# Two chained transformer blocks on one core: the value blocks of the memory, the filter products and the spectrum products each move one stage later

## The reference, cut to what matters

```python
# first block
x = x + 0.5 * rms(swiglu(rms(x, ffn1_pre_g), ffn1_w_gu, ffn1_w_down), ffn1_post_g)    # D_FF = 2816
...                                     # mixer: projections w_in (dt, xbc, q, k, v, z, gates) of rms(x, mix_pre_g),
mixed = (g_attn * attn_out + g_ssd * ssd_out) @ w_mix_out
x = x + rms(mixed, mix_post_g)
hq = rms(x, xa_pre_g)
qx = (hq @ xa_w_q)                                                     # 4 heads of 256
kx, vx = split(rms(mem, mem_norm_g) @ xa_w_kv, 2)                      # mem: 256 rows of 1024, an input
p = softmax(einsum('bqhd,bkhd->bhqk', qx, kx) * 256 ** -0.5)
x = x + rms(einsum('bhqk,bkhd->bqhd', p, vx) @ xa_w_o, xa_post_g)
x = x + 0.5 * rms(swiglu(rms(x, ffn2_pre_g), ffn2_w_gu, ffn2_w_down), ffn2_post_g)
# second block (Hyena and latent attention)
h = sin(freq_2 * (sin(freq_1 * (z @ w_f1 + b_f1)) @ w_f2 + b_f2))      # z: fixed positions
k = (h @ w_f3) * decay                                                 # filter taps, inputs alone
k_spec = rfft(both directions of k)                                    # used by the long convolution of Hyena
```

## Time and profile before

| | |
|---|---|
| median of 3 runs | 1103.66 us (1103.06 to 1103.74) |
| the profiled execution's own time | 1102.39 us |
| its span, first to last instruction | 1100.6 us |
| PE busy | 1085.5 us, 99% of the span, 8538 matmuls |
| DVE busy | 792.8 us, 72% |
| ACT busy | 590.7 us, 54% |
| the 16 DMA engines | 171 GB/s in the mean, 188.59 MB |
| mean granted TensorE clock | 1.000 |

### The profile page before, as it was taken

One profiled execution on the slowest core, in us unless ns is written; L12 is line 12 of the kernel. 1 busy time (PEld: TensorE's weight loads), 2 busy tenths in 40 slices (PEclk: granted clock), 3 DMA queues, 4 the chain that ended last, 5 costly groups with the idle time before them and its releaser, 6 DMA issues.

```text
span 1100.6 us, 21007 instructions
## 1 busy us (share of the span) xinstructions
PE 1085.5 (99%) x8538; PEld 1029.8 (94%) x8538; DVE 792.8 (72%) x1114; ACT 590.7 (54%) x844; POOL 0.2 (0%) x4
## 2 busy tenths in 40 slices
PE   9999999999999999999999999999999999999998
PEld 7999999999999999999999898999999798999998
DVE  5765555858998968777777867675555686997774
...
PEclk9999999999999999999999999999999999999999
...
DMA packets 29137, 188.59 MB, mean 171 GB/s; under 512 B 3496, under 2 KB 4809, under 8 KB 7370
## 3 DMA queue, kind: packets, MB, share of 16 engines
...
...
## 4 chain that ended last, share of the span: by engine, by line
PE 84%; DVE 9%; ACT 4%; issue 2%; DMA 1%; SPq 0%; ACTq 0%; DVEq 0%
PE bank L515 14%; PE bank L514 14%; PE bank L516 14%; PE bank L526 10%; PE bank L527 10%; PE bank L528 10%; DVE sb_w_lo L2017 3%; PE bank L613 2%; ACT sb_w_hi L1331 2%; PE bank L857 1%; PE bank L739 1%; PE bank L687 1%; DVE sb_hT_lo L2094 1%; DMA sb_w_raw<-in_w 1%; PE bank L1178 1%
## 5 line engine op out<-in xcount | busy, mean ns | idle before, releaser
L2017 DVE TENSOR_TENSOR sb_w_lo<-sb_w_raw,sb_w_hi 128x2048 fp32r<-128x2048 f32 x169 | 386.5, 2290 | 152.3 <-ACT sb_w_hi L1331 152.0
L1331 ACT ACTIVATE sb_w_hi<-sb_w_raw 128x2048 fp32r<-128x2048 f32 x169 | 322.8, 1910 | 34.5 <-PE bank L516 33.0
L514 PE MATMUL bank<-sb_hT_hi,sb_w_hi 128*128 128x256 f32 (+1 forms) x816 | 225.9, 277 | 0.0
L516 PE MATMUL bank<-sb_hT_hi,sb_w_lo 128*128 128x256 f32 (+1 forms) x816 | 225.8, 277 | 0.0
L515 PE MATMUL bank<-sb_hT_lo,sb_w_hi 128*128 128x256 f32 (+1 forms) x816 | 225.7, 277 | 0.0
L526 PE MATMUL bank<-sb_hT_hi,sb_w_hi 128*128 128x256 f32 (+2 forms) x744 | 213.4, 287 | 2.1 <-DVE sb_w_lo L2017 1.1
L527 PE MATMUL bank<-sb_hT_lo,sb_w_hi 128*128 128x256 f32 (+2 forms) x744 | 206.3, 277 | 0.0
L528 PE MATMUL bank<-sb_hT_hi,sb_w_lo 128*128 128x256 f32 x744 | 206.0, 277 | 0.0
L514 PEld LDWEIGHTS bank<-sb_hT_hi,sb_w_hi 128*128 128x128 f32 (+1 forms) x816 | 152.7, 187 | 0.1
L516 PEld LDWEIGHTS bank<-sb_hT_hi,sb_w_lo 128*128 128x128 f32 (+1 forms) x816 | 152.7, 187 | 0.1
L515 PEld LDWEIGHTS bank<-sb_hT_lo,sb_w_hi 128*128 128x128 f32 (+1 forms) x816 | 152.6, 187 | 0.1
...
## 6 DMA issues: line engine op xcount, KB each, us to landing
...
```

The source lines that it names most:

```text
L514: pe.matmul(o, a_hi, b_hi, start=first, stop=False)
L516: return pe.matmul(o, a_lo, b_hi, start=False, stop=last)
L1331: act.activation(w_hi[b % STAGES][:], w_raw[b % RING][:], ACT.Copy).then_inc(w_hi_in, 1)
L2017: tt(w_lo[b % STAGES][:], w_raw[b % RING][:], f32(w_hi[b % STAGES][:]), ALU.subtract).then_inc(w_lo_in, 1)
```

## The change

- **Weight list and keys.** The stage xa_kv of 8 blocks becomes xa_k (4 blocks, after FFN1) and xa_v (4 blocks, between mix_out and xa_q). After FFN1 PE runs kv0, kv1, kv2, `norm_turn(2)`, kv3, dt. The value blocks kv4 to kv7 stand after mix3, two on either side of `raw_turn(3)`.
- **Memory kept.** After the key blocks' hi and lo parts are used, a DVE add (128 x 2048) writes mem_T = hi + lo, and ACT waits for it before the copy of dt. In the first mixer, ahead of mix_out, ACT rounds it to late_hi and DVE subtracts to late_lo.
- **Filter.** The eight filter products move from the seam mix to xa to the seam xa to FFN2; all eight spectrum products from there and from after FFN2 to the seam FFN2 to second mixer, six ahead of `raw_turn(5)` and two behind it.
- **DVE.** `norm_rows(1)` moves from behind tile 3 of FFN1 to between tiles 20 and 21. The folds leave the cross attention: `filter_fold(0, 0..3)` stand behind tiles 0, 1, 2, 3 of FFN2 (in place of `spectrum_pair(0, *)`), `filter_fold(1, 0..2)` between tiles 20 and 21, `filter_fold(1, 3)` behind 21. In the second mixer `norm_low(6)` and `low_after(ckv)` come ahead of `spectrum_pair(1, *)`, and `spectrum_pair(0, *)` stands after `low_after(z_hy + 3)`.
- **Order after FFN1 on DVE.** Lower kv2, `norm_rows(2)`, lower kv3, `norm_low(2)`, lower dt, the add of mem_T, lower xbc0. Before it was: lower kv2 and kv3, `norm_rows(2)`, lower kv4 to kv7, `norm_low(2)`, lower the rest.
- **Small ones.** The load of the transform matrix (dft_f) on ACT's queue moves behind `post_gain(3)`; half buffers and dft_f lie elsewhere; `WIDER` has other entries.

Cut to its core (a line of "..." marks what is left out):

```diff
     ffn(1)
-    plain("xa_kv", "xa_w_kv", 0, 8)
+    plain("xa_k", "xa_w_kv", 0, 4)
...
     plain("mix_out", "w_mix_out", 0, 4)
+    plain("xa_v", "xa_w_kv", 4 * 256, 4)
     plain("xa_q", "xa_w_q", 0, 4)
...
-WIDER = {**dict.fromkeys(("xbc1", "xbc10", "qkv1", "qkv7", "gate0", "gate2", "gate3", "gate4", "ssd5", "attn3.0", "zz3",
-                          "gg6", "gg7", "hyo1.0"), (2, 2)),
-         **dict.fromkeys(("kv5", "qkv8", "qkv9", "qkv10", "gate6", "ssd7", "xaq2", "xaq3", "hy4"), (8, 8)),
-         "ckv": (2, 0), "xo2": (8, 0), "out2": (8, 0)}
+WIDER = {**dict.fromkeys(("xbc1", "xbc10", "xbc11", "qkv1", "gate0", "gate2", "gate3", "gate4", "ssd5", "ssd7", "attn3.0",
+                          "zz3", "gg6", "gg7", "hyo1.0"), (2, 2)),
+         **dict.fromkeys(("qkv9", "qkv10", "xaq2", "xaq3"), (4, 4)),
+         **dict.fromkeys(("qkv7", "qkv8", "gate6", "hy4"), (8, 8)),
+         "xo2": (4, 0), "ckv": (8, 0), "out2": (4, 0)}
...
         mem_lo = place(90, "mem_lo", [P, KD, SEQ], F32R)
+        mem_T = place(8, "mem_T", [P, KD, SEQ])
+        late_hi = place(32, "late_hi", [P, KD, SEQ], F32R)
+        late_lo = place(40, "late_lo", [P, KD, SEQ], F32R)
...
-        dft_f = place(0, "dft_f", [P, 4, P])
-        half = place(32, "half", [P, 2, 4, HY])
+        dft_f = place(56, "dft_f", [P, 4, P])
+        half = [place(0, "half0", [P, 4, HY]), place(40, "half1", [P, 4, HY])]
...
-            for i in range(8):
-                if i < 4:
-                    feature_block(f"kv{i}", FIRST["xa_kv"] + i, 2, mem_hi, mem_lo, ready=None if i else norm_done(1))
-                else:
-                    token_block(f"kv{i}", FIRST["xa_kv"] + i, 256, mem_hi, mem_lo)
-                if i == 4:
+            for i in range(4):
+                feature_block(f"kv{i}", FIRST["xa_k"] + i, 2, mem_hi, mem_lo, ready=None if i else norm_done(1))
+                if i == 2:
                     norm_turn(2, mix_xn, 2)
...
-            xq = FIRST["xa_q"]
-            for i in range(6):
-                filter_taps(i, (3, 4, 5, 6, xq % 3, (xq + 1) % 3)[i])
+            def value_block(h):
+                if h == 0:
+                    pe.wait_ge(S("late_lo"), 1)
+                token_block(f"kv{4 + h}", FIRST["xa_v"] + h, 256, late_hi, late_lo)
+            value_block(0)
+            value_block(1)
             raw_turn(3, x_added(1))
-            for i in (6, 7):
-                filter_taps(i, (xq + 2) % 3 if i == 6 else (xq + 1) % 3)
-            for i in range(8):
+            value_block(2)
+            value_block(3)
+            for i in range(4):
                 wait_read(pe, f"kv{i}")
...
-            filter_spectrum(0, (3, 4, 5, 6))
+            up = FIRST["ffn2"]
+            for i in range(6):
+                filter_taps(i, (3, 4, 5, 6, up % 3, (up + 1) % 3)[i])
             raw_turn(4, x_added(2))
+            for i in (6, 7):
+                filter_taps(i, (up + 2) % 3 if i == 6 else (up + 1) % 3)
             ffn_part(2, 4)
-            filter_spectrum(1, (0, 1, 2, 7))
+            at = (0, 1, 2, 7, (FIRST["cq"] + 1) % 3, (FIRST["cq"] + 2) % 3)
+            for i in range(6):
+                filter_spectrum(i, at[i])
             raw_turn(5, x_added(3))
+            for i in (6, 7):
+                filter_spectrum(i, at[i - 2])
...
-            for i in range(8):
-                if i == 2:
+            for i in range(4):
+                if i == 1:
                     act.wait_ge(S("x_ready"), X_READY[0] - 2)
                     norm_squares(x, mix_xn)
                 o = full(act, f"kv{i}")
-                if i < 4:
-                    copy(f"kv{i}", xa_k[:, 2 * i:2 * i + 2, :], two(o))
-                else:
-                    copy(f"kv{i}", xa_v[:, :, (i - 4) * 256:(i - 3) * 256], two(o))
-                after(FIRST["xa_kv"] + i)
-                if i == 4:
+                copy(f"kv{i}", xa_k[:, 2 * i:2 * i + 2, :], two(o))
+                after(FIRST["xa_k"] + i)
+                if i == 2:
                     norm_high(2, "mix_pre_g", hT_hi)
             o = full(act, "dt")
+            act.wait_ge(S("mem_T"), 1)
             copy("dt", ssd_dtF[:], o[0:SSD_HEADS, 0:SEQ])
...
             after(FIRST["attn_out"] + 3)
+            act.activation(late_hi[:], mem_T[:], ACT.Copy).then_inc(S("late_hi"), 1)
             hidden_sin(1)
...
-            for i in range(6):
-                taps(i)
+                copy(f"spec{n}.{f}", half[n][:, f, :], o[:])
+            def values(h):
+                o = full(act, f"kv{4 + h}")
+                copy(f"kv{4 + h}", xa_v[:, :, h * 256:(h + 1) * 256], two(o))
+                after(FIRST["xa_v"] + h)
+            values(0)
+            post_gain(2, POST[2])
+            norm_squares(x, xa_xn)
+            values(1)
             norm_high(3, "xa_pre_g", hT_hi)
-            for i in range(6, 8):
-                taps(i)
-            post_gain(2, POST[2])
-            norm_squares(x, xa_xn)
+            values(2)
+            values(3)
...
-            act.dma_start(dft_f[:].rearrange("p w f -> p (w f)"), a["c_dft"][:, 512:1024]).then_inc(S("dft_f_in"), 16)
             out_part("xa_o", "xo", 2)
-            for i in range(4):
-                spectrum(i)
+            for i in range(6):
+                taps(i)
             act.wait_ge(S("x_ready"), X_READY[2] - 2)
             norm_squares(x, ffn[2]["xn"])
             norm_high(4, "ffn2_pre_g", hT_hi)
+            for i in range(6, 8):
+                taps(i)
             post_gain(3, POST[3])
+            act.wait_ge(S("post_ssq"), POST_SSQ[2])
+            act.dma_start(dft_f[:].rearrange("p w f -> p (w f)"), a["c_dft"][:, 512:1024]).then_inc(S("dft_f_in"), 16)
             ffn_part(2)
-            for i in range(4, 8):
+            for i in range(6):
                 spectrum(i)
             norm_high(5, "g_norm_2", sec_hi)
+            for i in range(6, 8):
+                spectrum(i)
             after(down_at(2, PAIRS - 1))
...
+            def filter_fold(t, step):
+                k = kfil[:, t, :].rearrange("p (n w d) -> p n w d", n=2, w=2)
+                ahead, behind = k[:, :, 0, :], k[:, :, 1, :]
+                if step < 2:
+                    if step == 0:
+                        for i in range(4 * t, 4 * t + 4):
+                            wait_read(dve, f"taps{i}")
+                        dve.wait_ge(S("decay_in"), 16)
+                    src = (ahead, behind)[step]
+                    link(tt(src, src, decay[:, FOLD[t][step], :].unsqueeze(1).to_broadcast([P, 2, HY]), ALU.mult))
+                elif step == 2:
+                    dif = tt(kdif[:, t], ahead, behind, ALU.subtract)
+                    if t:
+                        dif.then_inc(S("folded"), 1)
+                        return
+                    link(dif)
+                    ts(kdif[0:1, t], behind[0:1], -1.0, None, ALU.mult).then_inc(S("folded"), 1)
+                    dve.wait_ge(S("folded"), 1)
+                    dve.wait_ge(S("bias_in"), 16)
+                    link(dve.tensor_copy(behind[0:1], bias_row[:]))
+                else:
+                    tt(ahead, ahead, behind, ALU.add).then_inc(S("folded"), 1)
+            def spectrum_pair(n, imag):
+                at = 2 * imag
+                for i in range(2):
+                    wait_read(dve, f"spec{n}.{at + i}")
+                e, o = half[n][:, at, :], half[n][:, at + 1, :]
+                tt(spec[:, n, at, :], e, o, ALU.add).then_inc(S("spec_on"), 1)
+                tt(spec[:, n, at + 1, :], o if imag else e, e if imag else o, ALU.subtract).then_inc(S("spec_on"), 1)
...
                 wait_read(dve, f"rb{n}")
                 hidden_tile(0, [], [b])
+                if n == 2:
+                    filter_fold(0, 0)
                 hidden_tile(1, [], [b + 1])
                 if n == 2:
-                    spectrum_pair(0, 0)
+                    filter_fold(0, 1)
                 hidden_tile(2, [b + 2], [b + 3])
                 if n == 2:
-                    spectrum_pair(0, 1)
+                    filter_fold(0, 2)
                 hidden_tile(3, [], [b + 4])
-                if n == 1:
-                    dve.wait_ge(S("mem_in"), 16)
-                    norm_rows(1, mem_xn, mem_xn, f["xn"])
+                if n == 2:
+                    filter_fold(0, 3)
                 with dve.Fori(0, PAIR_TURNS) as turn:
                     hidden_tile(4, [b + 5], [b + 6], turn)
                     hidden_tile(5, [], [b + 7], turn)
                 lowered[0] += 5 + TURN * PAIR_TURNS
                 b = lowered[0]
                 hidden_tile(FF_TILES - 2, [b], [b + 1])
+                if n == 1:
+                    dve.wait_ge(S("mem_in"), 16)
+                    norm_rows(1, mem_xn, mem_xn, f["xn"])
+                else:
+                    for step in range(3):
+                        filter_fold(1, step)
                 hidden_tile(FF_TILES - 1, [], [b + 2] if n == 1 else [])
+                if n == 2:
```

(22 more changed lines are left out.)

39 lines of the change are left out of this document (8 added, 31 removed).

## The result

The changed kernel takes 1108.88 us (median of 5 runs, 1107.99 to 1109.75) against 1103.1 (1103.03 to 1103.74) for the kernel before: +5.8 us, ratio 1.0051, 95% interval 1.0036 to 1.0066. Slower, as forecast: the interval is clear of 1, though the change is far under 2%. The median lies inside the stated range and 1.7 us above the stated number; the change itself is 5.8 us where 3.5 were forecast. The profiled execution took 1108.56 us with a span of 1106.8, 6.2 more than before. The metric's 0.5% is small, so each part is read from starts in the trace and not from medians alone. A pause "by the starts" is the distance of two starts less the usual step between such matmuls (0.11 us for 256 columns, 0.23 for 512).

The account below looks back on a forecast made before the run. The prediction took PE, busy for 99% of the span, as the bound, so only its work and pauses count. Its terms summed to +3.5 us, giving a median of 1107.2 us, range 1103.0 to 1110.5.

Parts of the forecast that it names:

- a: Head of FFN1: the delay from norm_rows(1) ahead of tile 4 goes, -1.0 us.
- b: Tail of FFN1: norm_rows(1) ahead of tile 21 makes PE stand 3.8 us before the memory's transposes, +3.5 us.
- c: FFN1 to first mixer: PE waits about 1.6 us each at dt and xbc0, less 0.7 for slower step, +2.5 us.
- d: mix_out and cross attention: value blocks gain nothing; a pause goes as the fold leaves DVE, -0.4 us.
- e: Cross attention to FFN2: longer filler of filter products removes three pauses and the slower step after them, -2.8 us.
- f: Head of FFN2: folding t = 0 on DVE makes pauses of 0.7, 0.7 and 0.5 us, +1.6 us.
- g: Tail of FFN2: three fold steps delay tile 21's lo part; PE stands 2.4 to 2.5 us, +2.5 us.
- h: FFN2 to second mixer: more filler shrinks waits for x and lo part, zz2's wait grows 0.7, -2.4 us.
- rival 1: Clock falls behind FFN1-tail pause, at most doubling the last down block (+5.4 us); 1109 to 1112.6 us, chance 0.12.
- Rival 2: FFN1-to-mixer pauses do not come, or issue step falls after pauses; 3.2 us less, 1104.0 us, chance 0.24.
- Rival 3: Vector work at both FFN tails is hidden, so 6.0 us vanish; 1101.2 us, chance 0.14.
- The range for the WIDER entries: Issue-step entries changed in 12 places, each up to 0.22 us either way: nothing in sum, 2.6 for range.

Follow-up runs that it names:

- e1: Changed kernel with norm_rows(1) back in its old place behind tile 3 of FFN1; 1108.0 us, ratio 1.0045.
- e8: Kernel before with only norm_rows(1) moved to between tiles 20 and 21 of FFN1; 1107.98 us, ratio 1.0044.
- e2: Changed kernel with norm_rows(1) split: squares behind tile 3 of FFN1, root and scaling between tiles 20 and 21; 1108.53 us, ratio 1.0049.
- e9: Changed kernel with 14 throwaway 512-column matmuls in PE's pause ahead of the memory's transposes; 1109.13 us, ratio 1.0055.
- e3: Changed kernel with the add of mem_T ahead of norm_low(2) instead of behind dt's lowering; 1109.58 us, ratio 1.0054.
- e10: Changed kernel with the moves of e1, e3, e4 and e5, plus ACT's norm_high(2) ahead of rounding dt's block; 1100.04 us, ratio 0.9976.
- e6: Changed kernel with the WIDER entries of the kernel before; 1112.06 us, ratio 1.0082.
- e4: Changed kernel with FFN2's fold of t = 1 spread: one step ahead of tile 20, one before 21, two behind; 1108.32 us, ratio 1.0048.
- e5: Changed kernel with spectrum_pair(1, *) ahead of cq1's lowering in the second mixer; 1108.53 us, ratio 1.0049.
- e11: e10 with spectrum_pair(1, *) back behind ckv's lowering; 1102.24 us, ratio 0.9986.
- e12: e10 with the three fold steps back between tiles 20 and 21 of FFN2; 1102.2 us, ratio 0.999.

## Why the prediction was right, and where its sizes were off

The actual terms are the differences of PE's starts between the two profiles at the ends of each part, with the moved work taken out. But for rounding they add up to the 6.2 us of the spans.

| part | predicted | profile |
|---|---|---|
| a head of FFN1 | -1.0 | -0.9 |
| b tail of FFN1 | +3.5 | +4.9 |
| c FFN1 to mixer | +2.5 | +2.8 |
| d cross attention | -0.4 | -0.5 |
| e cross attention to FFN2 | -2.8 | -2.3 |
| f, g FFN2 | +4.1 | +3.9 |
| h FFN2 to second mixer | -2.4 | -1.8 |
| sum | +3.5 | +6.2 |

- **b is the term that was mis-sized.** The pause came as worked out (3.8 predicted, 3.87 by the starts) and so did its cause (e1, e8). What the sum lacked is the clock: I held its fall to be a rival of 0.12 with a price of up to 5.4 us. It fell in all seven profiles with this pause, and it cost 1.3 to 2.3 us (8.78 to 9.77 us from the transposes to kv0 against 7.50 in e2 and e9), since it was back before the last down block was far. So rival 1's mechanism was right and its price too high by a factor of about three; it belonged in the forecast with 1.4. By the prediction's own signs it is rival 1 that came, beside the pauses: the clock is under 1.00, and the first 512-column matmuls of the last down block start 0.58 and 0.42 us apart where the later ones start 0.23 apart. All five runs of the changed kernel have a mean clock of 0.997 or 0.998, so it was no accident of one execution. That the median stays below rival 1's 1109 is a matter of its price. The price was also read from the wrong rows: the windows of the execution before print a granted clock of 1.00 for its first microseconds too, so nothing there shows that the 0.95 us of the earlier trace rows are those of a lowered clock. The Trainium skill ("TensorE: Matmul & The Clock Gate", section "Why this matters for your kernels") warns of an idle stretch between bursts; the 3.71 us row and the 0.69 behind it agree, and e9 shows the cause. What its "Part 4: PE-mode transpose" says of transposes is neither borne out nor refuted: in e2 the same transposes stood behind 2.44 us of idle time and the clock held.
- **c** was right in both waits: 1.44 and 1.64 by the starts for 1.6 and 1.6. The 0.7 us taken off for the slower step came only as 0.3, which is why the part measured 2.8. Rival 2 (norm_low follows ACT closely and DVE makes up mem_T) is refuted; e3 shows that DVE is what xbc0 waits for, e10 that it is what dt waits for.
- **f and g** were right: pauses of 0.80, 0.50 and 0.51 for 0.7, 0.7 and 0.5, and 2.40 for 2.4 to 2.5. Rival 3 is refuted at both tails by the rows at 188.96 and 873.45.
- **e** removed all three waits; half a microsecond less was gained than taken, since the issue step did not improve with them. **h** removed the wait for x, but zz2's wait grew by 1.5 where I had put 0.7: the chain of two inverse roots and the scalings stands whole behind the spectrum steps, so all of their delay arrives.
- **d**: nothing was gained or lost at the seam from mix_out, as said.
- The range for the WIDER entries (nothing in the sum) was right for a list made for the new order; e6 shows that leaving the old list would have cost about 2 us by the issue step.

The median lies 5.8 us above the one before, while each single move off the changed kernel (e1, e3, e4, e5) changed it by +0.7 to -0.9 us only. Their traces show each wait gone, and e11 and e12 show that such a wait alone in a kernel is paid for. Two things stand against the single moves. One is the issue step of a list that was not made for them. The other can be counted from the mean clock of every run: the changed kernel's profile with its one fall has 0.998, e2's with two has 0.997, e3's with a long and a short one has 0.995. One of the changed kernel's five runs is at 0.997 or less, but five of e3's and four of e4's, so these two kernels had a fall more in most of their runs. In e1 and e5 it is two of five.

Among the runs at 0.998 alone the changed kernel has a median of 1108.7 us (four runs), e5 1107.2 (three), e1 1105.9 and 1108.0, e4 1107.6 (one). So at equal falls the single moves gain more than their medians say, but the runs are few and lie up to 2.5 us apart. What sets where the step turns slow, and why with two or three long pauses left nearly every run has a fall at one of them, stays open.
